# An RWKV-7 / Mamba-2 / HGRN2 encoder step on one core: four order changes in the RWKV tile, and the finest HGRN level built from the gate

## The chip, the core and the metric

One Trainium2 chip, one of its cores. The metric is the device time of one launch in microseconds (us). TensorE is called PE, VectorE DVE, ScalarE ACT, GpSimd POOL and SyncE SP, as in the profile.

## What is computed

Two layers over a prompt of 1,024 tokens and 8 sample sequences of 16 tokens (1,152 columns, nine tiles of 128; the ninth holds the samples). Layer 0 mixes with RWKV-7 and Mamba-2 side by side, layer 1 with HGRN2; each mixer is followed by a gated feed-forward block. The change touches the RWKV scan and the HGRN2 block:

```python
def rwkv7_scan(r, decay, k, v, kk, a, s0):      # per token
    sa = einsum('bhvk,bhk->bhv', s, -kk_t)
    s = s * d_t + sa[..., None] * (kk_t * a_t) + v_t[..., None] * k_t
    o_t = einsum('bhvk,bhk->bhv', s, r_t)

def hgrn2_mixer(p, s0, lb, norm_w, chunk):
    log_f = log(lb + (1 - lb) * sigmoid(f))
    k = (1 - lb) * sigmoid(-f)                  # so exp(log_f) = 1 - k
    o = gla_chunked(silu(q), k, i, log_f, s0, chunk)

def gla_chunked(q, k, v, log_f, s0, chunk):
    seg = bcum[l] - bcum[s]                     # bcum: running sum of log_f
    att[l, s] = sum_k q[l] * k[s] * exp(seg)    # s <= l
```

## The kernel before

The stages follow one another: modulation, input projection of layer 0, RWKV (about 560 to 925 us of the span), Mamba-2, output projection, feed-forward, input projection of layer 1, HGRN2 (about 2,550 to 2,850 us), output projection, feed-forward, final norm. In every stage each engine runs a list written out by hand, strictly in order; semaphores alone join the lists. What an engine does in which order is thus the order of the calls in its loop.

**RWKV.** The loop over tiles is a pipeline of three: in step t the engines work on the solve of tile t, the state and output of tile c = t-1, and the gates and keys of tile u = t+1. Names that matter:
- `tilde(u)` (DVE, L2338 to 2345) makes the scaled operands AR, kt and bt; its semaphore `tilde_done` releases `grams(t)` on PE (L2510), which multiplies bt with AR (L2518), AR with bt (L2523) and, after `bonus_done`, kt with AR (L2529).
- `mask_grams(t, True)` (DVE) masks the first two products; `square(t)` (PE, L2536 through the helper `product`) squares them; `take_powers(t)` (ACT, L2069) copies the squares out of PSUM. `mask_grams(t, False)` masks the key product (L2278) and then adds the identity (L2283, semaphore `T0_done`). `fourth(t)` on PE needs the identity sum, the copies and, since it writes over banks 2 and 3, the masked key product.
- `solve(c, 0)` (PE, L2623) and its copy `take_U(c, 0)` (ACT, L2064) belong to the tile before; ACT issues `take_U` ahead of `take_powers`.
- Five additions `add_T` (DVE, L2290) build the inverse. Between the second and third of them DVE does `finish(c-1)` (L2369 to 2375) and `keys(u)` (L2308, L2310).
- `tokens(t)` (PE, L2569) turns v, b and k; `take_tokens(t)` (ACT, L2080) copies the three in that order under one semaphore, `tok_done`. `state_rows(c, 1)` (PE, L2615) and `lora(u)` (PE, L2472) wait for it.
- `bonus_key(u)` (DVE, L2335) needs POOL's `kmod`; `add_o(c)` (L2357), `unit_k(u)` (L2328) and `centre(c)` (L2361, L2364) follow it. `unit_k` waits for ACT's `exps(u)` (L2114, L2116), which stands behind ACT's copies of the second cross product (L2086).

**HGRN2.** Attention inside a tile is split in levels 64, 32, 16, 8, 4, 2, 1. For a level m, ACT exponentiates sums of log_f that PE makes (`exponents`, L3847; `decays`, L3583) into the buffer E, in groups of three arrays: rem, cum, 64; then 32, 16, 8; then 4, 2, 1. DVE multiplies the lower half of each pair by k and the upper by q (`level`, L3707, two instructions), and PE multiplies that array with itself (`far_of`, L3873; `gram_of`, L3891). DVE picks the scores with masks (`far_scores`, `scores` L3745, `near_scores` L3755); `outputs` on PE (L3932, L3934) needs them. `turn_gate(u)` (L3966) waits until all of group three is exponentiated; then come ACT's copy (L3589), DVE's `low_part` (L3676), and with `lf_low` PE's exponents of the next tile. DVE's list for a tile reads: three levels, `new_state` (L3765), `finish(c)` (L3783, L3787), `level(t, 4)`, `far_scores`, `low_part`, `scores(t, 0)`, `level(t, 2)`, `level(t, 1)`, `scores` 1 to 3, `near_scores`.

SP loads k and q of tile u into `kqg[:, u % 2]` once `KQ_done`, `Qe_done` and `gram0` say that tile u-2 is through with them. After the last prompt tile POOL builds V_e (L3661, eight instructions) in the same buffer, behind the same three semaphores.

## Time and profile before

| | |
|---|---|
| median of 3 runs | 3790.82 us (3788.09 to 3794.73) |
| profiled execution, its own time | 3792.62 us |
| its span | 3790.6 us |
| PE busy | 3557.4 us, 94% |
| DVE busy | 2127.6 us, 56% |
| ACT busy | 1059.7 us, 28% |
| POOL busy | 1417.3 us, 37% |
| mean granted PE clock | 0.972 |

The busy shares are averages over stages with different limits. In a timeline row the first number is the start from the beginning of the span, the second the time until the group of instructions ends, and the bracket the idle time of that engine ahead of the group with the instruction that ended it. Groups overlap by a little because an engine starts an instruction before the last one has drained.

### The profile page before, as it was taken

What the parts mean: (1) busy time and instruction counts of PE and PEld (TensorE: products, weight loads), DVE (VectorE), ACT (ScalarE), POOL (GpSimd) and SP (SyncE); (2) the same over time, 40 slices, a digit from 0 to 9 for tenths busy, and PEclk for the clock granted to TensorE, in tenths of its full rate; (3) what the DMA queues carried; (4) which work ended last, traced back from release to release, by engine and by line L of the source; (5) the groups of instructions that cost most, each with busy time, mean ns of one, the idle gap of its engine ahead of it and who ended that gap; (6) DMA issues with size and microseconds to landing.
All of it is one profiled execution on the core that took longest, in us unless ns stands there. A gap on an engine that the chain in (4) does not pass through costs nothing. (4 is left out here: it accounts for less than half of the span.)

```text
span 3790.6 us, 69437 instructions
## 1 busy us (share of the span) xinstructions
PE 3557.4 (94%) x29702; PEld 3351.9 (88%) x29702; DVE 2127.6 (56%) x2992; ACT 1059.7 (28%) x1751; POOL 1417.3 (37%) x1140
## 2 busy tenths in 40 slices
PE   7999988888898999999999999988879899999998
PEld 6999967777668899999999999987769799999998
DVE  5543656664694675555644635337765855555446
ACT  2000114553551143333200224015540433332100
POOL 4222221210003367777533322230013577776331
PEclk8999999998899999999999999999999999999999
DMA  6454441001432112222322123223341122223322
GB/s 219 163 183 168 165 129 31 23 23 30 97 82 76 32 61 73 70 70 70 120 92 76 49 100 126 94 90 105 86 132 48 44 72 70 74 72 98 104 89 73
DMA packets 393333, 339.27 MB, mean 90 GB/s; under 512 B 19827, under 2 KB 363377, under 8 KB 386910
## 3 DMA queue, kind: packets, MB, share of 16 engines
q1 hardware_dynamic: 381712, 290.89, 25.0%
q10 hardware_dynamic: 11214, 44.33, 2.9%
q8 instruction: 215, 3.52, 0.4%
q0 software_dynamic: 128, 0.00, 0.2%
q14 instruction: 64, 0.52, 0.0%
HBM read 249.95 MB, written 85.24 MB: 88 GB/s over the span
## 5 line engine op out<-in xcount | busy, mean ns | idle before, releaser
L1301 PE MATMUL ffn_acc<-ffn_BH,ffn_WH 128*128 128x384 f32 x1232 | 418.8, 340 | 23.5 <-DVE ffn_BL L1511 12.6
L1301 PE MATMUL ffn_acc<-ffn_BL,ffn_WH 128*128 128x384 f32 x1232 | 417.0, 338 | 0.0
L1301 PE MATMUL ffn_acc<-ffn_BH,ffn_WL 128*128 128x384 f32 x1232 | 416.5, 338 | 0.0
L1238 POOL TENSOR_TENSOR ffn_WL<-raw,ffn_WH 128x512 fp32r<-128x512 f32 x176 | 282.3, 1606 | 261.5 <-ACT ffn_WH L1387 261.5
L1728 PE MATMUL ffn_acc<-ffn_BH,ffn_WH 128*128 128x384 f32 x1056 | 354.0, 335 | 6.7 <-DVE ffn_BL L1792 4.3
L1728 PE MATMUL ffn_acc<-ffn_BL,ffn_WH 128*128 128x384 f32 x1056 | 353.6, 335 | 0.0
L644 PE MATMUL in_ab_acc<-hH,in_ab_wH 128*128 128x384 f32 (+2 forms) x840 | 289.0, 344 | 5.1 <-DVE hL L502 5.1
L1238 POOL TENSOR_TENSOR ffn_WL<-ffn_S,ffn_WH 128x512 fp32r<-128x512 f32 x176 | 274.5, 1570 | 33.0 <-ACT ffn_WH L1387 33.0
L644 PE MATMUL in_ab_acc<-hL,in_ab_wH 128*128 128x384 f32 (+2 forms) x840 | 285.5, 340 | 0.0
L644 PE MATMUL in_c_acc<-hH,in_c_wH 128*128 128x384 f32 (+1 forms) x768 | 261.0, 340 | 6.9 <-DVE hL L502 6.8
L1301 PEld LDWEIGHTS ffn_acc<-ffn_BH,ffn_WH 128*128 128x128 f32 x1232 | 234.1, 190 | 30.9 <-POOL ffn_WL L1238 15.1
L644 PE MATMUL in_c_acc<-hL,in_c_wH 128*128 128x384 f32 (+1 forms) x768 | 260.7, 339 | 0.0
L1301 PE MATMUL ffn_acc<-ffn_hH,ffn_WH 128*128 128x394 f32 x704 | 239.8, 341 | 4.8 <-DVE ffn_hL L1543 4.3
L1301 PE MATMUL ffn_acc<-ffn_hH,ffn_WL 128*128 128x394 f32 x704 | 240.8, 342 | 0.0
L1301 PE MATMUL ffn_acc<-ffn_hL,ffn_WH 128*128 128x394 f32 x704 | 240.5, 342 | 0.0
L1728 PE MATMUL ffn_acc<-ffn_BH,ffn_WL 128*128 128x384 f32 x1056 | 240.4, 335 | 0.0
L1801 DVE SCALAR_TENSOR_TENSOR xT<-ffn_acc,mod,xT 128x768 f32<-128x768 f32 x96 | 97.6, 1016 | 254.3 <-PE ffn_acc L1728 254.3
L1301 PEld LDWEIGHTS ffn_acc<-ffn_BL,ffn_WH 128*128 128x128 f32 x1232 | 234.3, 190 | 0.0
L1301 PEld LDWEIGHTS ffn_acc<-ffn_BH,ffn_WL 128*128 128x128 f32 x1232 | 234.2, 190 | 0.0
L1728 PEld LDWEIGHTS ffn_acc<-ffn_BH,ffn_WH 128*128 128x128 f32 x1056 | 198.7, 188 | 7.9 <-DVE ffn_BL L1792 4.9
L1728 PEld LDWEIGHTS ffn_acc<-ffn_BL,ffn_WH 128*128 128x128 f32 x1056 | 198.7, 188 | 0.0
L644 PE MATMUL in_ab_acc<-hH,in_ab_wL 128*128 128x384 f32 (+2 forms) x840 | 196.6, 339 | 0.0
(629 smaller groups left out, 8210.7 us busy)
## 6 DMA issues: line engine op xcount, KB each, us to landing
in_ab_ada<-in_ada_w SPq DMA_DIRECT2D x40, 1024.0 KB, 5.0
hidden<-ffn_up SPq DMA_DIRECT2D x44, 576.0 KB, 2.8
raw<-in_w_gate SPq DMA_DIRECT2D x44, 512.0 KB, 3.7
raw<-in_w_up SPq DMA_DIRECT2D x44, 512.0 KB
raw<-in_w_down SPq DMA_DIRECT2D x80, 256.0 KB, 2.6
pT<-in_ab_out ACTq DMA_DIRECT2D x34, 576.0 KB, 3.2
pT<-in_c_out ACTq DMA_DIRECT2D x32, 576.0 KB, 3.7
raw<-in_w_in_ab SPq DMA_DIRECT2D x34, 512.0 KB, 4.5
```

What stands on the lines that cost most here:

```text
L644: ins = self.nc.tensor.matmul(self.acc[0:rows, u, c, 0:n], w[:, u, k, 0:rows], x[:, k, c * CH:c * CH + n], start=(k == 0 and w is self.wH ...
L1238: self.nc.gpsimd.tensor_tensor(self.WL[:, slot], src, self.WH[:, slot].bitcast(F32), ALU.subtract).then_inc(lo, 1)
L1301: ins = self.nc.tensor.matmul(self.acc[:, bank, 0:n], w[:, slot, k, :], x(low, k), start=start and k == 0 and w is self.WH and low == 0, s ...
L1728: ins = nc.tensor.matmul(acc[:, pair + c if c < 2 else third, 0:CH], w[:, slot, k, :], x[:, k, chunk(c)], start=k == 0 and w is m.WH and x ...
L1801: stt(xs, acc[:, pair:pair + 2, 0:CH], gate[:, n, 0:1], xs, ALU.mult, ALU.add)
```

## The change

In RWKV, DVE makes bt before kt, with a semaphore of its own for kt (`keys_done`), adds the identity before it masks the key product, and from tile 2 on does `bonus_key` after `add_o` (for tile 1 after `unit_k`). ACT copies the squares before `take_U(c, 0)`. The copy of v gets a semaphore (`v_copied`), for which `state_rows(c, 1)` now waits.

In HGRN2 the third group has two arrays. Level 1 is built by one DVE instruction as (1 - k) q in the upper half, and its product takes k itself as the other operand. Since k is thus read until that product is done, SP's load and POOL's V_e wait for `gram_mm` as well.

```diff
-            def take_powers(t):
+            def take_squares(t):
                 for q in range(2):
                     act.wait_ge(S1_mm, 2 * t + q + 1)
                     copy(flat4(pw[:, q, 0:2, :, :]), bank[:, q, :]).then_inc(S1_out, 1)
+
+            def take_powers(t):
...
-                for dst, b in ((v_tok, 6), (b_tok, 2), (k_tok, 3)):
-                    ins = copy(dst[:, t % 2, :, :, :].rearrange("p j q k -> p (j q k)"), bank[:, b, :])
-                ins.then_inc(tok_done, 1)
+                copy(tokens_of(v_tok), bank[:, 6, :]).then_inc(v_copied, 1)
+                copy(tokens_of(b_tok), bank[:, 2, :])
+                copy(tokens_of(k_tok), bank[:, 3, :]).then_inc(tok_done, 1)
...
+                if 0 <= t <= LAST:
+                    take_squares(t)
                 if 0 <= c < LAST:
                     take_U(c, 0)
...
-                tt(kt[:, :, :], kmod[:, :, :], c_[:, :, :], ALU.mult)
                 dve.wait_ge(ba_done, u + 1)
                 tt(bt[:, :, :], a_[:, :, :], c_[:, :, :], ALU.mult).then_inc(tilde_done, 1)
+                tt(kt[:, :, :], kmod[:, :, :], c_[:, :, :], ALU.mult).then_inc(keys_done, 1)
...
                 if front:
                     decay(u)
-                if front and u:
-                    bonus_key(u)
...
                 if 0 <= c <= LAST:
                     add_o(c)
+                if front and u > 1:
+                    bonus_key(u)
                 if front:
                     unit_k(u)
-                if u == 0:
+                if front and u <= 1:
                     bonus_key(u)
...
                 ins.then_inc(A_mm, 1)
+                pe.wait_ge(keys_done, t + 1)
                 pe.wait_ge(bonus_done, t + 1)
...
                 if s == 1:
-                    pe.wait_ge(tok_done, min(c + 2, NT))
+                    pe.wait_ge(v_copied, min(c + 2, NT))
...
-        GROUPS = (("rem", "cum", 64), (32, 16, 8), (4, 2, 1))
-        LAST_GROUPS = (("rem", "cum", 8), (4, 2, 1))
+        GROUPS = (("rem", "cum", 64), (32, 16, 8), (4, 2))
+        LAST_GROUPS = (("rem", "cum", 8), (4, 2))
...
                     sp.wait_ge(gram0, u - 1)
+                    sp.wait_ge(gram_mm, 4 * (u - 1))
...
             pool.wait_ge(gram0, NTP)
+            pool.wait_ge(gram_mm, 4 * NTP)
...
+            def level_1(t):
+                dve.wait_ge(E_done, NP * t + PAIRS_ * len(groups_of(t)))
+                v, k, q = (halves(x, 1)[1] for x in (buffer_of(t, 1), k_[:, t % 2], q_[:, t % 2]))
+                stt(v, k, 1.0, q, ALU.subtract, ALU.mult, reverse0=True).then_inc(KQ_done, 1)
...
-                            ins = mm(bank[:, b + h % 2, 0:3 * P], lf_tok[:, part, h, :], sums_r[:, at:at + 3, :],
+                            ins = mm(bank[:, b + h % 2, 0:n * P], lf_tok[:, part, h, :], sums_r[:, at:at + n, :],
...
+                keys_ = k_[:, t % 2] if FINE[i] == 1 else KQ
```

DVE's list in step t of RWKV from the key product on, before (`act` holds the powers and masked products, `mixer_shared` the state S):

```order
L2296 TENSOR_TENSOR sumsq<-sumsq,rwkv_bank 64x512
L2278 TENSOR_TENSOR act<-rwkv_bank,rwkv_mask_k 128x512 x2
L2283 TENSOR_TENSOR act<-act 128x256 x2
L2290 TENSOR_TENSOR act<-act,rwkv_bank 128x256 x2
L2301 TENSOR_TENSOR mixer_shared<-mixer_shared,rwkv_bank 128x256
```

and of the change:

```order
L2301 TENSOR_TENSOR sumsq<-sumsq,rwkv_bank 64x512
L2283 TENSOR_TENSOR act<-act 128x256 x2
L2287 TENSOR_TENSOR act<-rwkv_bank,rwkv_mask_k 128x512 x2
L2295 TENSOR_TENSOR act<-act,rwkv_bank 128x256 x2
L2306 TENSOR_TENSOR mixer_shared<-mixer_shared,rwkv_bank 128x256
```

The identity sums (L2283 in both) have moved ahead of the two key masks. ACT's list at the same place, before:

```order
L2064 COPY rwkv_Ut<-rwkv_bank 64x512
L2069 COPY act<-rwkv_bank 128x512 x2
L2072 COPY rwkv_W<-rwkv_bank 128x512 x2
L2075 COPY act<-rwkv_bank 128x256 x2
L2090 ACTIVATE rwkv_tanh_in<-act 64x128
```

and of the change:

```order
L2069 COPY act<-rwkv_bank 128x512 x2
L2064 COPY rwkv_Ut<-rwkv_bank 64x512
L2074 COPY rwkv_W<-rwkv_bank 128x512 x2
L2077 COPY act<-rwkv_bank 128x256 x2
L2093 ACTIVATE rwkv_tanh_in<-act 64x128
```

The two copies of the squares (L2069) now stand ahead of the copy of U.

## Rows read from the trace of the kernel before

**Rows 1.** Busy time by stretch: RWKV's steady tiles, and most of HGRN2.
```profile
604.70:900.00 295.30, 261.63 (x6594) 230.56 (x6591) 194.55 (x357) 148.58 (x312) 51.19 (x42) 1.00 0.08 22
...
2500.00:2800.00 300.00, 261.43 (x4793) 232.58 (x4793) 195.68 (x347) 139.10 (x163) 29.17 (x54) 0.97 0.34 100
```
**Rows 2.** Timeline of PE, a steady RWKV tile.
```profile
682.29 1.10 PE L2518 MATMUL rwkv_bank<-rwkv_AR,rwkv_bt 64*64 64x128 f32 x32 [0.86 <-DVE rwkv_bt L2345]
...
687.52 1.09 PE L2623 MATMUL rwkv_bank<-sumsq 64*64 64x64 f32 x16
689.81 0.39 PE L2536 MATMUL rwkv_bank<-act 64*64 64x64 f32 x6 [1.20 <-DVE act L2283]
...
698.80 0.68 PE L2615 MATMUL rwkv_bank<-mixer_shared,rwkv_AR 64*64 64x64 f32 x16 [0.67 <-ACT rwkv_k_tok L2080]
...
700.50 0.68 PE L2584 MATMUL rwkv_bank<-act 64*64 64x64 f32 x16
...
719.88 1.10 PE L2518 MATMUL rwkv_bank<-rwkv_AR,rwkv_bt 64*64 64x128 f32 x32 [0.86 <-DVE rwkv_bt L2345]
```
**Rows 3.** Timeline of DVE, the same tile, first half.
```profile
681.56 0.68 DVE L2345 TENSOR_TENSOR rwkv_bt<-raw 128x512 f32<-128x512 f32 x1
...
687.00 1.27 DVE L2278 TENSOR_TENSOR act<-rwkv_bank,rwkv_mask_k 128x512 f32<-128x512 f32 x2
688.20 0.74 DVE L2283 TENSOR_TENSOR act<-act 128x256 f32<-128x256 f32 x2
...
695.65 0.42 DVE L2290 TENSOR_TENSOR act<-act,rwkv_bank 128x256 f32<-128x256 f32 x1 [0.51 <-PE rwkv_bank L2536]
...
699.81 0.74 DVE L2290 TENSOR_TENSOR act<-act,rwkv_bank 128x256 f32<-128x256 f32 x2
```
**Rows 4.** Timeline of ACT, the same stretch.
```profile
681.01 0.84 ACT L2134 COPY sumsq<-rwkv_bank 128x256 f32<-128x256 f32 x2 [2.91 <-PE rwkv_bank L2599]
...
688.65 0.58 ACT L2064 COPY rwkv_Ut<-rwkv_bank 64x512 f32<-64x512 f32 x1 [3.08 <-PE rwkv_bank L2623]
689.13 1.06 ACT L2069 COPY act<-rwkv_bank 128x512 f32<-128x512 f32 x2
...
697.09 0.58 ACT L2080 COPY rwkv_v_tok<-rwkv_bank 128x512 f32<-128x512 f32 x1 [1.14 <-PE rwkv_bank L2569]
```
**Rows 5.** Timeline of DVE, second half of the tile.
```profile
710.75 2.13 DVE L2335 SCALAR_TENSOR_TENSOR rwkv_columns<-rwkv_columns,colB,rwkv_kmod 128x128 f32<-128x128 f32 x4 [1.10 <-POOL rwkv_kmod L2245]
...
714.16 0.69 DVE L2328 TENSOR_TENSOR rwkv_kk<-rwkv_kk,rwkv_sq 128x512 f32<-128x512 f32 x1 [0.68 <-ACT rwkv_sq L2116]
```
**Rows 6.** Timeline of ACT and POOL, second half of the tile.
```profile
710.48 0.58 ACT L2129 COPY rwkv_o<-rwkv_bank 128x512 f32<-128x512 f32 x1 [2.91 <-PE rwkv_bank L2658]
...
710.67 1.27 POOL L2235 TENSOR_TENSOR raw<-raw 128x512 f32<-128x512 f32 x1
```
**Rows 7.** Timeline of DVE, a steady HGRN tile.
```profile
2637.09 1.29 DVE L3707 TENSOR_TENSOR hgrn_E<-hgrn_E,hgrn_kqg 128x512 f32<-128x512 f32 x2 [0.58 <-ACT hgrn_E L3583]
...
2639.55 1.21 DVE L3676 TENSOR_TENSOR hgrn_lf_tok<-hgrn_bank,hgrn_lf_tok 128x1024 fp32r<-128x1024 f32 x1
```
**Rows 8.** Timeline of PE and ACT, the same HGRN tile.
```profile
2635.54 1.51 ACT L3583 ACTIVATE hgrn_E<-hgrn_bank 128x768 f32<-128x768 f32 x2 [0.63 <-PE hgrn_bank L3847]
...
2640.81 1.66 PE L3847 MATMUL hgrn_bank<-decay_sums,hgrn_lf_tok 128*128 128x384 f32 x8 [0.25 <-DVE hgrn_lf_tok L3676]
```
**Rows 9.** Timeline of DVE, level 4 of the first HGRN tile.
```profile
2576.11 1.29 DVE L3707 TENSOR_TENSOR hgrn_E<-hgrn_E,hgrn_kqg 128x512 f32<-128x512 f32 x2 [2.98 <-ACT hgrn_E L3583]
```
**Rows 10.** Timeline of POOL and DVE at the end of HGRN.
```profile
2788.32 4.61 POOL L3661 TENSOR_TENSOR hgrn_kqg<-raw,row_half 128x256 f32<-128x256 f32 x8 [246.60 <-DVE hgrn_E L3707]
2793.08 1.80 DVE L3755 COPY_PREDICATED act<-act 32x256 f32<-32x256 uint32 x4
...
2816.67 4.96 DVE L3755 COPY_PREDICATED act<-act 32x256 f32<-32x256 uint32 x4
2817.21 4.12 POOL L3667 TENSOR_TENSOR hgrn_late<-hgrn_late,act 128x1024 f32<-128x1024 f32 x2 [24.28 <-PE hgrn_bank L3948]
```

27 lines of the change are left out of this document (15 added, 12 removed).

## The prediction

> **What bounds the kernel now.** I read first the busy time by stretch, then the timelines of the two stages that the change touches, engine by engine, looking in each for the wait that ends last. The change touches nothing outside RWKV (about 560 to 925 us) and HGRN2 (about 2,550 to 2,850 us), so everything else is carried over as it is. In both stages PE is the busiest engine but not full: 262 of 295 us in the steady RWKV tiles, 261 of 300 in HGRN2 [rows 1]. PE waits there for chains through DVE and ACT, and only the waits on such a chain are worth anything.
>
> A steady RWKV tile takes 719.88 - 682.29 = 37.6 us from one gram product to the next [rows 2]; there are seven of them (tiles 1 to 7). PE has three waits in the first half: 0.86 us ahead of L2518 for bt, 1.20 us ahead of L2536 at 689.81, and 0.67 us ahead of L2615 for the last token copy [rows 2]. From 700.50 on PE runs without a gap up to the second cross product, then come ACT's copy of it, its Ln and its Exp, and from 714.16 DVE is the chain up to bt [rows 5].
>
> An HGRN tile takes about 28.8 us. The chain that I find is DVE's: it stands 0.58 us for the last exponential of group three, then does level 4, the far scores and `low_part`; PE stands 0.25 us for `low_part` [rows 7, 8]. From there PE's exponents and grams, DVE's near scores, PE's outputs and ACT's copy lead back to DVE.
>
> **RWKV, edit by edit (steady tile).**
>
> *bt before kt.* bt is finished one operation of 0.60 us earlier, at 681.64 instead of 682.24 [rows 3]. But the grams also need R to be copied out of banks 0 and 1, and these copies end at 681.01 + 0.84 = 681.85 [rows 4]. The new wait takes the place of the old one: L2518 starts near 681.9, gain 0.4 us (bounds 0 and 0.6). The key product stands behind `bonus_done` as before, and kt is ready before that, so `keys_done` costs nothing; if bonus were sooner, kt would end 0.6 us ahead of it still.
>
> *Identity first and squares before U, together.* What held PE until 689.81 was the last of three things: the identity sum, finished at 688.94 [rows 3], and the first copy of the squares, finished at 689.13 + 0.58 = 689.71 because ACT had waited until 688.65 for U [rows 4]. PE had its square products done by about 687.7, since it started the solve at 687.52 [rows 2]; with the copies in front both are out by about 688.3, before U is there at 688.65, so U is not delayed. On DVE the identity sums take 687.00 to 687.7 and the first key mask is done near 688.4, half of the 1.27 us later [rows 3]. PE is busy with the solve until 689.81 - 1.20 = 688.6 [rows 2]. So the fourth power can start at 688.6: gain 1.2 us (bounds 0.8, should the second key mask at 689.0 hold it, and 1.3). Each edit alone would give less: without the ACT edit the wait stays at 689.71.
>
> *`v_copied`.* L2615 needs only v, copied by 697.67 [rows 4], and can start when PE is through with the third product, 0.67 us before 698.80 [rows 2]. `lora` still waits for the last copy, which ended just before 698.80, so it starts there instead of 0.6 us later, behind L2615. But the cross product that follows needs the third addition on DVE, which starts at 699.81 because DVE had 3.7 us of `finish` and `keys` since 696.07 [rows 3]; the first half of it is there near 700.23. So L2584 moves from 700.50 to 700.28: gain 0.2 us (bounds 0 and 0.8).
>
> *`bonus_key` after `add_o`.* DVE waited 1.10 us for kmod and then took 2.13 us for four instructions, which end at 712.88 [rows 5]. POOL's L2235 runs from 710.67 to 711.94 [rows 6]. Moved, they come behind an addition of about 0.7 us that waits for ACT's copy of o, done at 711.06 [rows 6], and can start at 711.8. `unit_k` waits for ACT until 714.16 anyway. I cost the move at nothing; the cover is the 1.3 us between 712.88 and 714.16, and should the four instructions last their 2.13 us from 711.8, they end at 713.9, just inside. The mean comes 1.3 us earlier but DVE takes it only after `unit_k`. Bounds: 1.0 us lost if the cover goes, 0.6 gained.
>
> Per steady tile 0.4 + 1.2 + 0.2 = 1.8 us, seven times 12.6 us. In tile 8 the first two terms hold and the third does not (extra matmuls fill PE there): 1.6 us. In tile 0 there is no U; bt and the identity are worth about 0.9, and for u = 1 `bonus_key` now comes behind `unit_k` (0.6 us), with POOL running against it: about 0.5 lost, net 0.4. **RWKV: 14.6 us less.**
>
> **HGRN2, edit by edit.**
>
> *Group three with two arrays.* PE's eight matmuls of 384 columns took 1.66 us [rows 8]; 256 columns should leave 1.66 minus at most a third (0.55), at least nothing. I take 0.43, which is 8 times 128 columns at 2.4 GHz, the level of the granted 1.00 there. The exponential of 768 elements was 0.8 us (two in 1.51); a copy of 512 elements out of PSUM takes 0.58 [rows 4, 8], so 0.2 less for the one that ends last. The last exponential of the group comes 0.43 + 0.43 + 0.2 = 1.06 us earlier. DVE waited only 0.58 us for it [rows 7], then it is bound by its own list (`finish` before level 4). So a steady tile gains 0.58 us, and PE's other 0.5 us turn into a longer wait for `low_part`. Seven tiles: 4.1 us. In tile 0 there is no `finish` and DVE waited 2.98 us [rows 9]: the whole 1.06 counts.
>
> The Trainium skill (TensorE: Matmul & The Clock Gate, Back-to-back issue gap) gives a sustained spacing of about 81 ns at 128 columns and 131 ns at 512; by that rule 128 columns would be worth about 17 ns a matmul, 0.13 us per eight, the exponential would come 0.46 us earlier and a steady tile would gain 0.46, not 0.58 us. The row speaks for a steeper price, since eight matmuls of 384 columns in 1.66 us are some 0.17 us apart, beyond the page's figure for 512.
>
> *Level 1 by one instruction instead of two.* One DVE instruction of 0.6 us less, but in steady tiles DVE then waits for PE's last gram; covered by PE. In the last tile, where DVE leads, it and the smaller group give about 0.6 us. The product with k as the other operand costs the same number of matmuls.
>
> *The later load of k and q.* It is issued about 2.5 us later and needed a tile later: nothing.
>
> *V_e.* POOL's eight instructions (0.61 us each, 4.61 in all) ran 2788.32 to 2792.93, while DVE's near scores, on the chain, came at 2793.08 and took 1.80 us [rows 10]. Now POOL starts when the last gram is done, at the same moment as the near scores. One case shows what that costs: at 2816.67 the same four instructions took 4.96 us beside POOL's L3667 [rows 10]. Bounds 0 and 3.2 us, once; I take 2.4, four waits of one POOL instruction (0.61) each. The Trainium skill (SBUF — State Buffer, Who interferes with whom) says that a DVE instruction with two SBUF inputs and a POOL instruction that reads SBUF block each other for a whole instruction; by that rule it is the 2.4, by the ratio of the two rows 3.2. Here the change speaks against itself.
>
> **HGRN2: 4.1 + 1.1 + 0.6 - 2.4 = 3.4 us less.** Sum 14.6 + 3.4 = 18.0 us. The profiled execution took 3792.6, so its like would be 3774.6; the median of the runs is 1.8 us lower, which gives **3773 us**. A measurement of this kernel can tell about 0.2% (7.6 us) from no change, so faster begins below 3783.2.
>
> **The rivals.**
> - *The next wait gives half of RWKV back.* For: every gain there was already cut by a successor 0.2 to 0.4 us behind (R's copies, the solve on PE, `keys` on DVE), and durations of the key masks are modelled. If the fourth power starts only after the second mask, and bt and v are worth nothing, a tile gains 0.8 instead of 1.8: 7 us less gain, 3780 us. Chance 0.15.
> - *PE is the bound after all.* For: PE is busy nine tenths of both stages. Then the HGRN tile gains its whole 1.06 (3.4 us more) and the earlier mean in RWKV is worth up to 0.5 a tile (4 us): 3766 us. Against: the bracketed waits for DVE. Chance 0.10.
> - *The edits do not bite.* The identity and the key mask only change places, both being needed, and V_e takes what HGRN gives: 0.4 a tile left, about 3787 us, no change. Against: the ACT order, a clear 1 us. Chance 0.08.
> - *Slower, by PE's clock.* The leaner HGRN tile leaves PE with longer waits (0.25 becomes about 0.7 us ahead of the next exponents). The granted clock was 0.97 in this stretch, so it does fall there at times [rows 1]; 0.5 (1.2 GHz) would double PE's work. If a third of each of the seven tiles (about 10 us) ran at the lower level, it would cost 5 us a tile, 35 us in all: 3808 us. It decides once it takes 25 us more than now, about 3.6 us a tile. The same page on the clock gate has the clock fall after an idle window; that rule would give this case, and so far the trace has no fall in the steady tiles, whose longest PE waits are 1.2 us. Chance 0.04.
>
> **How the numbers follow.** My case has 0.63, with a range of its own of 3767 to 3780. With the first two rivals, faster is 0.88, same 0.08, slower 0.04. The range 3762 to 3784 takes in the first two rivals and the bounds of the RWKV terms, and leaves out the last two.
>
> **What would show it.** In the new profile: L2518 waiting for R's copies rather than bt; ACT's L2069 ahead of L2064 and the wait ahead of the fourth power gone; the RWKV tile at 35.8 us; the HGRN tile at 28.3 us with DVE's 0.58 us wait gone and PE's wait for `low_part` grown to about 0.7; near scores of the last prompt tile near 4 us beside V_e. I am wrong if the RWKV tile stays above 36.7 us, if the HGRN tile is a full microsecond shorter, or if the granted clock falls in steady tiles.

## Result, and the profile after

The changed kernel took 3762.61 us, median of the runs beside which the kernel before took 3792.06 us (four, 3788.09 to 3794.73). The ratio is 0.992, with a 95% interval of 0.9906 to 0.9934. (One of the changed kernel's four executions was disturbed, at a granted clock of 0.77, and is left out of the ratio.) So the gain was 29.5 us where 18.0 were forecast; 3762.61 lies at the very edge of the range (3762 to 3784), and 29.5 us less than the 3790.82 from which the forecast started would be 3761.3, outside it. Over every execution of this study the kernel before averages 3790.9 us (47 of them, 3781.2 to 3799.2) and the changed one 3763.5 (13, 3759.1 to 3770.4): a difference of 27.4 us, with a standard error of about 1.0. A single pair of profiles can be off by several microseconds either way, and much below turns on that.

The page of the changed kernel, its first lines:

```profile
span 3760.5 us, 69444 instructions
...
PE 3537.9 (94%) x29702; PEld 3338.3 (89%) x29702; DVE 2118.6 (56%) x2983; ACT 1053.5 (28%) x1751; POOL 1417.9 (38%) x1140
```

PE is busy 19.5 us less, DVE 9.0, ACT 6.2. Busy time fell by less than the span (30.1 us).

**The RWKV tile.** PE's timeline of a steady tile, answering to [rows 2] (start, duration, engine, line, operation, tiles, and in brackets the idle time ahead with what ended it):

```profile
677.55 1.10 PE L2523 MATMUL rwkv_bank<-rwkv_AR,rwkv_bt 64*64 64x128 f32 x32 [0.52 <-DVE rwkv_bt L2349]
...
682.77 1.09 PE L2629 MATMUL rwkv_bank<-sumsq 64*64 64x64 f32 x16
683.74 2.92 PE L2542 MATMUL rwkv_bank<-act 64*64 64x64 f32 x93
...
691.88 0.64 PE L2621 MATMUL rwkv_bank<-mixer_shared,rwkv_AR 64*64 64x64 f32 x14
692.72 0.34 PE L2477 MATMUL rwkv_bank<-rwkv_tanh_in,rwkv_w 64*128 64x128 f32 x1 [0.20 <-ACT rwkv_k_tok L2084]
```

All three waits of before have shrunk or gone: the one ahead of the first gram from 0.86 to 0.52 us, the 1.20 us ahead of the fourth power altogether, and the 0.67 us ahead of the cross product (L2621 now) has become 0.20 us in front of the low-rank products. The same tile on ACT and on DVE:

```profile
676.62 0.84 ACT L2137 COPY sumsq<-rwkv_bank 128x256 f32<-128x256 f32 x2 [2.90 <-PE rwkv_bank L2605]
...
681.58 0.58 ACT L2069 COPY act<-rwkv_bank 128x512 f32<-128x512 f32 x1 [0.40 <-PE rwkv_bank L2542]
682.98 0.58 ACT L2069 COPY act<-rwkv_bank 128x512 f32<-128x512 f32 x1 [0.82 <-PE rwkv_bank L2542]
683.90 0.58 ACT L2064 COPY rwkv_Ut<-rwkv_bank 64x512 f32<-64x512 f32 x1 [0.33 <-PE rwkv_bank L2629]
```

```profile
676.56 0.68 DVE L2349 TENSOR_TENSOR rwkv_bt<-raw 128x512 f32<-128x512 f32 x1
677.17 0.68 DVE L2350 TENSOR_TENSOR rwkv_kt<-rwkv_kmod,raw 128x512 f32<-128x512 f32 x1
...
682.24 0.75 DVE L2283 TENSOR_TENSOR act<-act 128x256 f32<-128x256 f32 x2
682.91 1.27 DVE L2287 TENSOR_TENSOR act<-rwkv_bank,rwkv_mask_k 128x512 f32<-128x512 f32 x2
```

The bracket ahead of L2523 names DVE's bt, which ends at 677.24. ACT's second copy of R ends later, at 676.62 + 0.84 = 677.46, and PE starts at 677.55: the bracket names one of several semaphores, and the durations show which was last. The copies of the squares wait for PE alone now, the second done at 683.56, before the fourth power at 683.74.

**The HGRN tile.** I cut it in three on DVE: from the first addition into the state (L3765 before, L3780 after) to `low_part` (L3676, L3686), from there to the near scores (L3755, L3770), and on to the next addition. A steady tile before:

```profile
2631.96 2.15 DVE L3765 SCALAR_TENSOR_TENSOR hgrn_S<-hgrn_S,act,hgrn_bank 128x128 f32<-128x128 f32 x8
...
2646.54 1.80 DVE L3755 COPY_PREDICATED act<-act 32x256 f32<-32x256 uint32 x4
...
2660.80 2.15 DVE L3765 SCALAR_TENSOR_TENSOR hgrn_S<-hgrn_S,act,hgrn_bank 128x128 f32<-128x128 f32 x8
```

and after:

```profile
2607.25 2.15 DVE L3780 SCALAR_TENSOR_TENSOR hgrn_S<-hgrn_S,act,hgrn_bank 128x128 f32<-128x128 f32 x8
...
2611.72 1.29 DVE L3722 TENSOR_TENSOR hgrn_E<-hgrn_E,hgrn_kqg 128x512 f32<-128x512 f32 x2
...
2614.16 1.21 DVE L3686 TENSOR_TENSOR hgrn_lf_tok<-hgrn_bank,hgrn_lf_tok 128x1024 fp32r<-128x1024 f32 x1
...
2621.47 1.81 DVE L3770 COPY_PREDICATED act<-act 32x256 f32<-32x256 uint32 x4
...
2635.33 1.89 DVE L3780 SCALAR_TENSOR_TENSOR hgrn_S<-hgrn_S,act,hgrn_bank 128x128 f32<-128x128 f32 x7
```

With `low_part` at 2639.55 [rows 7] the parts were 7.59, 6.99 and 14.26 us; now they are 6.91, 7.31 and 13.86 us. The first part hardly varies in the steady tiles, 7.58 to 7.61 us in four profiles before and 6.90 to 6.92 after, since DVE no longer stands in front of level 4 (L3722). In the first period, where DVE waited 2.98 us [rows 9], it went from 7.59 to 6.48. The other two parts vary from tile to tile, 6.4 to 10.7 and 13.85 to 19.3 us: a second thing is at work there, which a section below takes up.

On PE the pieces of the forecast:

```profile
2609.38 1.21 PE L3862 MATMUL hgrn_bank<-decay_sums,hgrn_lf_tok 128*128 128x256 f32 x8
...
2614.41 0.75 PE L3907 MATMUL hgrn_bank<-hgrn_E 128*32 128x32 f32 x64 [0.40 <-DVE act L3748]
2615.42 1.68 PE L3862 MATMUL hgrn_bank<-decay_sums,hgrn_lf_tok 128*128 128x384 f32 x8 [0.26 <-DVE hgrn_lf_tok L3686]
```

Eight matmuls of 256 columns take 1.21 us, 0.45 less than of 384 [rows 8] (forecast 0.43). PE's wait for `low_part` stayed at 0.26 us; the half microsecond that was to lengthen it lies 1 us earlier, as a new 0.40 us wait for DVE's far scores.

**The end of HGRN2**, answering to [rows 10]:

```profile
2766.11 6.32 POOL L3671 TENSOR_TENSOR hgrn_kqg<-raw,row_half 128x256 f32<-128x256 f32 x8 [243.84 <-PE hgrn_bank L3907]
```

```profile
2766.46 2.82 DVE L3770 COPY_PREDICATED act<-act 32x256 f32<-32x256 uint32 x4
```

V_e and the near scores do run side by side, and both suffer: POOL's eight instructions 6.32 us instead of 4.61, DVE's four 2.82 instead of 1.80. The cost on the chain was 1.0 us, not 2.4.

### The profile page after: what moved, and what is told of

Read it like the earlier page. It is cut to its first block and busy times, and to the rows that moved or that the text cites. A ratio compares the mean times of both kernels' runs of the same rounds, so it can differ in the third digit from the quotient of the medians.

```text
span 3760.5 us, 69444 instructions
## 1 busy us (share of the span) xinstructions
PE 3537.9 (94%) x29702; PEld 3338.3 (89%) x29702; DVE 2118.6 (56%) x2983; ACT 1053.5 (28%) x1751; POOL 1417.9 (38%) x1140
## 3 DMA queue, kind: packets, MB, share of 16 engines
q1 hardware_dynamic: 381712, 290.89, 25.5%
## 5 line engine op out<-in xcount | busy, mean ns | idle before, releaser
L644 PE MATMUL in_ab_acc<-hH,in_ab_wH 128*128 128x384 f32 (+2 forms) x840 | 289.1, 344 | 5.1 <-DVE hL L502 5.1
L644 PE MATMUL in_ab_acc<-hL,in_ab_wH 128*128 128x384 f32 (+2 forms) x840 | 285.3, 340 | 0.0
L644 PE MATMUL in_c_acc<-hH,in_c_wH 128*128 128x384 f32 (+1 forms) x768 | 261.3, 340 | 6.8 <-DVE hL L502 6.8
L644 PE MATMUL in_c_acc<-hL,in_c_wH 128*128 128x384 f32 (+1 forms) x768 | 261.2, 340 | 0.0
L644 PE MATMUL in_ab_acc<-hH,in_ab_wL 128*128 128x384 f32 (+2 forms) x840 | 196.5, 339 | 0.0
```

The lines of the kernel that those rows point to most:

```text
L644: ins = self.nc.tensor.matmul(self.acc[0:rows, u, c, 0:n], w[:, u, k, 0:rows], x[:, k, c * CH:c * CH + n], start=(k == 0 and w is self.wH ...
```

## The part of the first 30 us that no edit explains

Against the same instructions in both first profiles, the change was 14.2 us ahead at RWKV's last grams and 15.5 at the transposes behind RWKV (L2914), which nothing in it touches. There (from before's L2914 to its L2938) the kernel before took 19.47 us and the changed one 15.29, so it was 19.7 us ahead. HGRN2's seven periods brought it to 24.8, and what lies behind them to 30.1. This gave two theories, **C**: the stretches of low granted clock fall differently in every execution, and **D**: it belongs to the edits.

## The experiments

### Each stage alone

`rwkv_only` has the RWKV part of the diff, `hgrn_only` the HGRN2 part.

> The RWKV edits alone, HGRN2 as before. My theory: the RWKV tile stays at 35.67 us as in the changed kernel, RWKV is 15.7 us shorter at tile 8's fourth power, and HGRN2 keeps its 28.85 us tile; the rest of what is gained comes from where PE's granted clock stands low between RWKV and Mamba-2, 4.5 us in the changed kernel, which may be here again or not. Sum 3771 to 3776 us (16 to 21 less than before). Rival: the gain outside the two stages belongs to the HGRN edits; then this is 16 us and hgrn_only has all the rest.

> The HGRN2 edits alone, RWKV as before. My theory: 6 us less in HGRN2 (the tile 28.85 to 28.1 us, 1.1 us in tile 0, V_e costs about 1), nothing before it, so 3784 to 3787 us; the stretch between RWKV and Mamba-2 stays as long as in the kernel before, since RWKV ends at the same time. If the gain of 3.6 us behind HGRN2 follows the clock's phase, it may differ from the changed kernel's. Rival: the sum of the two halves is far from the whole 29.5 us because the edits help each other: then this one gives less than 3 us or more than 10.

`rwkv_only`: 3774.47 us, ratio 0.9949 (0.9934 to 0.9964), against 3791.73 for the kernel before. RWKV tile 35.67 us. `hgrn_only`: 3778.36 us, ratio 0.9964 (0.9951 to 0.9977); RWKV tile 37.58 us. The two give 17.3 and 13.4 us, 30.7 together, so within their intervals (13.6 to 25.0 and 8.7 to 18.6 us) they add up. HGRN2's part, forecast at 3.4 and expected here at 6, is beyond its rival's bound of 10 and the larger surprise; its own profile has 9.4 us of it inside HGRN2. In `hgrn_only`'s profile L2914 to L2938 took 15.27 us although nothing ahead of it differs from the kernel before, the first sign for theory C.

### The group of three arrays back, all else changed

```diff
-        GROUPS = (("rem", "cum", 64), (32, 16, 8), (4, 2))
-        LAST_GROUPS = (("rem", "cum", 8), (4, 2))
+        GROUPS = (("rem", "cum", 64), (32, 16, 8), (4, 2, "spare"))
+        LAST_GROUPS = (("rem", "cum", 8), (4, 2, "spare"))
```

> The changed kernel, but PE and ACT still make and exponentiate the third array of group three, which nobody reads (DVE overwrites it with level 1 from the gate). My theory: DVE's wait of 0.58 us ahead of level 4 is back in each HGRN tile and the tile is 28.6 to 28.7 us, so the smaller group is worth 0.6 us a tile and the single DVE instruction almost nothing there. Rival (PE bound): the tile stays near 28.85, since PE's 0.9 us are back; rival (DVE's instruction count): it stays at 28.1.

One execution, 3771.41 us. DVE's timeline, a steady tile:

```profile
2639.60 2.15 DVE L3780 SCALAR_TENSOR_TENSOR hgrn_S<-hgrn_S,act,hgrn_bank 128x128 f32<-128x128 f32 x8
...
2644.73 1.29 DVE L3722 TENSOR_TENSOR hgrn_E<-hgrn_E,hgrn_kqg 128x512 f32<-128x512 f32 x2 [0.59 <-ACT hgrn_E L3592]
2647.20 1.21 DVE L3686 TENSOR_TENSOR hgrn_lf_tok<-hgrn_bank,hgrn_lf_tok 128x1024 fp32r<-128x1024 f32 x1
```

The wait is back (0.59 us, 0.58 before), and the first part of the tile is 7.60 us. The two-array group alone makes that part shorter; level 1 by one instruction, the other thing left in, does nothing to it. Four periods took 28.1 to 28.8 us, the three others 30.0 to 31.8.

### The two losing edits mended

```diff
-                if front and u > 1:
+                if front and u:
                     bonus_key(u)
...
-                if front and u <= 1:
+                if u == 0:
                     bonus_key(u)
...
-            pool.wait_ge(gram_mm, 4 * NTP)
+            pool.wait_ge(att_done, NTP)
```

> The changed kernel with two places mended: for tile 1 bonus_key stands ahead of unit_k as before, and POOL starts V_e only when the near scores of the last prompt tile are done. My theory: tile 0 of RWKV is about 1.5 us shorter, the last outputs of HGRN2 come 1.0 us earlier (near scores 1.8 instead of 2.8 us); 2.5 us less, 3760 us, if the low stretches of PE's clock fall alike. Rival: those stretches move with the shift and hide it: 3758 to 3766.

3760.29 us, ratio 0.9913 (0.9899 to 0.9926). RWKV's tile 0 took 33.49 us instead of 35.10, and the near scores of the last prompt tile 1.79 us again, with POOL behind them (its eight instructions took 7.43 us there, beside other work of DVE, and nothing waited for them). It was timed again at the end (below).

### The same kernels again: what one execution can show

> The kernel before, profiled a second time. What is disputed is the time outside the two changed stages: from RWKV's last products to Mamba-2 the change took 4.5 us less, and another 3.6 us after HGRN2, though no instruction differs there. Theory C (where the stretches of low granted clock fall differs from one execution to the next): the stretch from the first transposes behind RWKV (L2914) to the last ones (L2938) lasts anything from 15.3 to 19.5 us here, not 19.47 again, and the span differs from the first by up to 5 us. Rival D (the gain outside belongs to the edits): 19.47 us again within 0.3, span 3790.6 within 2.

> The changed kernel, profiled a second time. The stretch from L2914 to L2938 (before's numbering) took 15.29 us in its first profile. Theory C: anything from 15.3 to 19.5 us. Rival D: 15.3 within 0.3. Both expect RWKV tiles of 35.67 us within 0.05, and HGRN tiles whose irregular gaps (2.3 us in the fourth tile of the first profile) may lie in another tile.

> The changed kernel once more, in rounds beside the kernel before. The pairs of profiles differ: 30.1 us between the first two, 19.9 between the second two. Theory C (about 5 us of the first difference was where the low clock happened to fall): the difference of medians is 22 to 27 us. Rival (the 30 us are the change's): 28 to 31 us. Between: L2914 to L2938 (before's numbering) 15.3 us in most executions.

`before_again` 3784.91 us, `after_again` 3764.89; `after_third` 3766.06 us in the median, ratio 0.9934 (0.9913 to 0.9955). The stretch from L2914 to L2938, by window (us; PE, PEld, DVE, ACT, POOL busy with their instructions; granted PE clock, DMA share, GB/s), in the first profile before, in `before_again`, in the first after, and in `after_third`:

```profile
937.40:956.87 19.47, 17.25 (x91) 12.32 (x91) 5.05 (x6) 12.05 (x20) 0.00 (x0) 0.59 0.64 164
```

```profile
934.43:949.70 15.27, 12.10 (x90) 8.40 (x91) 5.05 (x6) 11.78 (x20) 0.00 (x0) 0.88 0.83 209
```

```profile
921.91:937.20 15.29, 12.10 (x90) 8.42 (x91) 5.06 (x6) 11.77 (x20) 0.00 (x0) 0.89 0.84 209
```

```profile
921.59:941.05 19.46, 17.25 (x91) 12.25 (x91) 5.06 (x6) 12.06 (x20) 0.00 (x0) 0.59 0.65 164
```

Both kernels have both cases: 15.3 us at a mean granted clock of 0.88, and 19.5 us at 0.59. The clock rows of the traces have two levels, 1.00 (2.4 GHz) and 0.5 (1.2 GHz), so about a quarter of the stretch was at the lower in the one case and four fifths in the other, and PE's 91 matmuls took 12.1 or 17.2 us. Theory C holds here, D falls. This stretch alone moved the first comparison by 4.2 us. What decides between the two cases is not shown.

### One RWKV edit undone at a time

All start from the changed kernel and have one execution each: `no_squares` 3780.07 us (3771 expected), `no_identity` 3766.02, `no_bt` 3765.89, `no_v` 3762.78, `old_bonus` 3759.02. The changed kernel's own executions lie from 3759.1 to 3770.4, so these times decide little, and I go by the RWKV tile. `no_squares`:

```diff
-                if 0 <= t <= LAST:
-                    take_squares(t)
                 if 0 <= c < LAST:
                     take_U(c, 0)
                 if 0 <= t <= LAST:
+                    take_squares(t)
                     take_powers(t)
```

> The changed kernel with ACT's copies of the squares behind U again, as before. My forecast gave the ACT order and the identity order 1.2 us together and said that neither works without the other. So: the wait ahead of the fourth power is back, near 1.1 us, ended by ACT, and the RWKV tile is 36.8 us (36.6 to 37.0), time 3771 us. Rival (the identity order alone carries it): tile 36.0 or less.

The RWKV tile took 37.00 us, 1.33 more, at the upper end of what was expected. (The time was 16.5 us above the changed kernel's mean where the tiles account for 9.2; 3.2 more are the stretch from L2914 to L2938, 19.50 us here.) PE's timeline, fourth power, where the wait has no semaphore in the bracket; ACT's shows what is late:

```profile
687.22 2.92 PE L2541 MATMUL rwkv_bank<-act 64*64 64x64 f32 x93 [1.20 <-issue]
```

```profile
686.06 0.58 ACT L2064 COPY rwkv_Ut<-rwkv_bank 64x512 f32<-64x512 f32 x1 [2.72 <-PE rwkv_bank L2628]
686.54 1.06 ACT L2069 COPY act<-rwkv_bank 128x512 f32<-128x512 f32 x2
```

The first square is out at 686.54 + 0.58 = 687.12, and PE starts at 687.22. The profile calls this wait "issue", but the engine that it waits for is ACT.

`no_identity` puts the masks of the key product ahead of the identity sums again:

```diff
-                dve.wait_ge(gram_out, 2 * t + 2)
-                for q in range(2):
-                    ins = tt(pw[:, q, 2, :, :], gram_b[:, b, q, :, 0, :], bc(eye[:, :], 1, PAIRS), ALU.add)
-                ins.then_inc(T0_done, 1)
                 for q in range(2):
                     dve.wait_ge(gram_k_mm, t + 1)
...
+                dve.wait_ge(gram_out, 2 * t + 2)
+                for q in range(2):
+                    ins = tt(pw[:, q, 2, :, :], gram_b[:, b, q, :, 0, :], bc(eye[:, :], 1, PAIRS), ALU.add)
+                ins.then_inc(T0_done, 1)
```

> The changed kernel with the identity sums behind the key masks again on DVE. My forecast: the fourth power then waits for the identity sum behind two masks of 1.27 us, as before near 1.2 us after PE is through with the solve: RWKV tile 36.7 us (36.3 to 36.9). Without squares first it was 37.00. Rival (ACT's order alone does it): 35.9 or less.

36.20 us, 0.52 more, below what I expected (36.7, with 36.3 as the lower bound): PE waits 0.38 us ahead of the fourth power, since the sums end soon after PE gets there.

```profile
685.30 2.95 PE L2542 MATMUL rwkv_bank<-act 64*64 64x64 f32 x93 [0.38 <-DVE act L2288]
```

Without the ACT order the DVE order seems to have no worth: both undone were not run, but what the other two edits leave of the whole 1.90 us (0.35 and 0.22, below) is the same 1.33. With the ACT order, the DVE order brings 0.52 of the 1.33.

`no_bt` has kt ahead of bt again, `no_v` lets the cross product wait for all three copies again:

```diff
+                tt(kt[:, :, :], kmod[:, :, :], c_[:, :, :], ALU.mult).then_inc(keys_done, 1)
                 dve.wait_ge(ba_done, u + 1)
                 tt(bt[:, :, :], a_[:, :, :], c_[:, :, :], ALU.mult).then_inc(tilde_done, 1)
-                tt(kt[:, :, :], kmod[:, :, :], c_[:, :, :], ALU.mult).then_inc(keys_done, 1)
```

```diff
-                    pe.wait_ge(v_copied, min(c + 2, NT))
+                    pe.wait_ge(tok_done, min(c + 2, NT))
```

> The changed kernel with kt ahead of bt again. My forecast: 0.4 us a tile, so 36.1 us (35.7 to 36.3), the wait ahead of the grams (L2518 in before's numbering) being for bt, 0.6 us later than now. Rival (the copies of R or of the identity chain hold it anyway): 35.7 to 35.8.

> The changed kernel with L2615 (before's numbering) waiting for all three token copies again. My forecast: 0.2 us a tile (bounds 0 and 0.8): RWKV tile 35.9 us. The other undone parts measured 37.00 without the ACT order, 36.20 without the DVE order, 36.03 without bt first, 35.69 with bonus_key at its old place, beside 35.68 changed and 37.58 before; 1.90 less 1.33 less 0.35 leaves 0.22 for this one. Rival (the cross product waits for the same copies anyway): 35.7.

36.03 us (0.35) and 35.90 us (0.22). PE's waits came back, here for the grams and for the cross product:

```profile
678.82 1.10 PE L2523 MATMUL rwkv_bank<-rwkv_AR,rwkv_bt 64*64 64x128 f32 x32 [0.87 <-DVE rwkv_bt L2350]
```

```profile
694.12 0.68 PE L2621 MATMUL rwkv_bank<-mixer_shared,rwkv_AR 64*64 64x64 f32 x16 [0.67 <-ACT rwkv_k_tok L2084]
```

`old_bonus` has `bonus_key` ahead of `add_o` again:

```diff
+                if front and u:
+                    bonus_key(u)
                 if c == LAST:
...
-                if front and u > 1:
-                    bonus_key(u)
                 if front:
                     unit_k(u)
-                if front and u <= 1:
+                if u == 0:
                     bonus_key(u)
```

> The changed kernel with bonus_key at its old place, ahead of add_o. My forecast costed the move at nothing in a steady tile and at 0.5 us lost in tile 0. So: RWKV tile 35.67 us within 0.1, DVE waiting about 1.1 us for kmod ahead of bonus_key again, and tile 0 shorter by 0.5 (forecast) or by about 2 us (what the trace of the changed kernel suggests: tile 0 took 35.10 us though 1 us was gained at its start). Rival (the later place delays unit_k or helps the mean): the tile changes by over 0.2 us either way.

35.69 us, as with the change: the move is worth nothing in a steady tile. Tile 0 took 33.78 us instead of 35.10. `bonus_key(1)` in the changed kernel, then here:

```profile
596.41 0.71 DVE L2333 TENSOR_TENSOR rwkv_kk<-rwkv_kk,rwkv_sq 128x512 f32<-128x512 f32 x1 [2.00 <-ACT rwkv_sq L2119]
597.05 3.15 DVE L2340 SCALAR_TENSOR_TENSOR act<-act,colB,rwkv_kmod 128x128 f32<-128x128 f32 x4
```

```profile
596.20 2.12 DVE L2340 SCALAR_TENSOR_TENSOR act<-act,colB,rwkv_kmod 128x128 f32<-128x128 f32 x4 [2.21 <-POOL rwkv_kmod L2250]
598.25 0.68 DVE L2333 TENSOR_TENSOR rwkv_kk<-rwkv_kk,rwkv_sq 128x512 f32<-128x512 f32 x1
```

It starts 0.85 us later, and its four instructions last 1.03 us longer. One by one they took 1.35, 1.35, 0.34 and 0.34 us in the changed kernel and 1.33, 0.34, 0.34 and 0.34 here: an instruction of 0.34 us that runs beside one of POOL's (L2240, L2253, 1.3 to 1.7 us) lasts a whole microsecond longer, and at the later place two of them do, not one. PE's bonus sums wait for them (L2509 at 600.26, at 598.38 here).

### What the irregular gaps in HGRN2 are

PE's waits in HGRN2's seven periods before have lines with "issue": idle time within a string of small matmuls for which no semaphore stands.

```profile
PE hgrn_bank L3891 <- issue: 3.9, 5, 2.2
...
PE hgrn_bank L3859 <- issue: 2.6, 4, 0.8
PE hgrn_bank L3847 <- issue: 2.4, 1, 2.4
```

With one more of 0.25 the gaps sum to 9.2 us there; in four profiles before 9.2, 11.0, 11.3 and 15.4, in four after 10.1, 11.1, 10.4 and 11.0. The seven periods lasted 205.7, 209.5, 211.0 and 213.8 us before. The largest gaps of the changed kernel come at the very same matmul in each of its four profiles, with 22 of a string's 64 left (first profile, then `after_fourth`):

```profile
2648.03 0.39 PE L3907 MATMUL hgrn_bank<-hgrn_E 128*32 128x32 f32 x22 [2.33 <-issue]
```

```profile
2647.13 0.39 PE L3907 MATMUL hgrn_bank<-hgrn_E 128*32 128x32 f32 x22 [2.32 <-issue]
```

The DMA view of the gap between, 2645.5 to 2648.1, shows a packet of the instruction queue among the load's:

```profile
q1 hardware_dynamic: 482, 0.24, 32.0%
q8 instruction: 1, 0.02, 2.3%
```

Two theories, both tried. **L**: the loads matter. The change's later load of k and q, which I had costed at nothing, parts them. The kernel before with that one wait added:

```diff
                     sp.wait_ge(gram0, u - 1)
+                    sp.wait_ge(gram_mm, 4 * (u - 1))
```

> The kernel before, and of the change only the one added wait on SP's queue in HGRN2: the load of k and q starts after the last gram. My forecast costed it at nothing: 3791 us, within 2 of the kernel before. New theory L: the load is where HGRN2 gained more than forecast. In the traces PE stands 0.6 to 3.8 us without a semaphore in strings of small gram matmuls, next to the 16 KB packets of the instruction queue q8, and most where these come while the loads run back to back (2.5 MB in 10 us). With the later load the 1.5 MB and the 1.0 MB come apart in every tile. By L the seven periods of HGRN (first add into the state to the eighth) fall from 205.7 to 210.7 us (three profiles with the old order) to about 204, and the time is 3 to 5 us less. An own effect of the new order beyond 6 us would surprise both.

3786.31 us, ratio 0.9991 (0.9981 to 1.0002), the kernel before 3789.49 beside it. The seven periods took 206.9 us where 204 were expected (the mean of four profiles before: 210.0), gaps 9.9 us, and the first part of the tile stayed at 7.59. In the time the interval holds no change. In the traces one gap settles more, the one between the matmuls of L3847 in the sixth period, in the kernel before and in `load_only`:

```profile
2736.24 0.62 PE L3847 MATMUL hgrn_bank<-decay_sums,hgrn_lf_tok 128*128 128x384 f32 x2 [2.40 <-issue]
```

```profile
2729.65 0.62 PE L3848 MATMUL hgrn_bank<-decay_sums,hgrn_lf_tok 128*128 128x384 f32 x2 [1.03 <-issue]
```

The 2.5 us ahead of these gaps, by window, before and in `load_only` (the last two numbers are the DMA share and GB/s):

```profile
2731.30:2733.80 2.50, 2.50 (x128) 2.18 (x127) 1.71 (x4) 0.49 (x2) 0.00 (x0) 1.00 1.14 343
```

```profile
2726.10:2728.60 2.50, 2.50 (x128) 2.17 (x127) 1.72 (x4) 0.22 (x1) 0.00 (x0) 1.00 0.20 38
```

(A packet that begins in the window counts whole, so the share can pass 1.) In all five profiles with the early load this gap is 2.40 to 3.77 us, in all fifteen with the later load 1.02 to 2.13; with RWKV's edits it stands five matmuls earlier in the string. So the later load shortens the gap of the sixth period; the sixth period of `load_only` took 29.67 us, those of the kernel before 30.7 to 33.9. For the other gaps it is not shown.

**I**: the gaps sit where packets of PE's instructions end. `shift64` was to add half a packet's worth of matmuls to tile 0:

```diff
-                        ins = mm(near_bank(4)[r, h, :], k_[:, t % 2, h, r], q_[:, t % 2, h, r], start=True, stop=True)
+                        for _ in range(3 if t == 0 else 1):
+                            ins = mm(near_bank(4)[r, h, :], k_[:, t % 2, h, r], q_[:, t % 2, h, r], start=True, stop=True)
```

> The changed kernel with each of the 32 first gram products (L3874) of HGRN2's tile 0 done three times: 64 matmuls more, 128 records of PE's instruction stream, half of a 16 KB packet, worth 2 to 3 us once at most. Theory I (the gaps in PE's strings without a semaphore sit where the instruction packets end): in three profiles of the changed kernel the periods that stand out are the fourth (30.1 to 31.3 us) and the sixth (29.4 to 30.3) of seven, the others near 28.0; here both go back to 28.5 or less, others may stand out instead, and the gap of 1.8 to 2.6 us in the fourth is gone. Rival (the gaps belong to loads or to tiles): fourth and sixth stand out again, by 1.5 us or more.

3768.63 us. The fourth period, 30.1 to 31.3 us in the changed kernel, took 27.62, and the gap of 2.3 us in it was gone. The sixth still stood out (29.48 us) with its gap of 1.86 us. Another gap of 3.08 us stood within the tripled string.

This run does not test I, because it shifted by a whole packet and not by half of one. The 64 extra products are 128 matmuls in the profile (29,830 instead of 29,702) and 128 weight loads more, and the instruction queue q8 moved 216 packets instead of 215. So the ends of the packets fell on the same matmuls as in the changed kernel, and so did the gaps: tile 0's stands with 6 of the string left in both, here of 2.37 us and there of 1.39 to 1.82 (first profile of the changed kernel, then `shift64`).

```profile
2561.79 0.26 PE L3907 MATMUL hgrn_bank<-hgrn_E 128*32 128x32 f32 x6 [1.39 <-issue]
```

```profile
2568.95 0.26 PE L3908 MATMUL hgrn_bank<-hgrn_E 128*32 128x32 f32 x6 [2.37 <-issue]
```

That the fourth period's gap was gone says nothing for the shift either: it was gone in `no_v` too (27.60 us), which adds no matmul.

What speaks for I is in the traces of the other runs. First, each of the 223 gaps above 0.2 us in the twenty profiles, the last prompt tile included, ends 1.2 to 1.6 us after a packet of 16 KB on q8 has landed; the sixth period's is no exception. Second, the gaps lie 127 or 128 matmuls apart or near a multiple of that (380, 508), and 128 matmuls with their weight loads are the 256 instructions that made one packet in `shift64`. Third, RWKV's edits move them though they touch nothing in HGRN2: tile 0's string had 2 matmuls left in the kernel before, in `hgrn_only` and in `load_only`, and 6 in `rwkv_only` and the changed kernel, and the fourth period's 18 left in `hgrn_only`,

```profile
2662.71 0.35 PE L3901 MATMUL hgrn_bank<-hgrn_E 128*32 128x32 f32 x18 [2.00 <-issue]
```

and 22 in the changed kernel. (The wait for `keys_done`, nine of them, would by my estimate shift the stream by nine instructions, four to five pairs of matmul and weight load.) So in these traces a gap stands only where a packet ends. How long it is at such a place, from nothing to 3.8 us, depends on the load in one case and is open in the others.

**What follows a large gap.** Within the seven periods PE's clock fell to its lower level for 3.4 us (once for 6.8), once or twice in each of the four profiles of each kernel. Each time it fell within a gap of 1.8 to 2.95 us or at most 1.6 us behind its end: at 2585.3 us in the first profile before, at 2649.1 in the first after, where the gap of 2.33 us ends at 2648.03. Other gaps as long had no fall behind them. Its price shows in the sixth period of `after_again` and of `after_fourth`, with the same gap of 1.85 us: the third part took 15.43 us at the full clock and 17.05 with such a stretch. Taking the gaps and half of the time at the lower clock from the seven periods leaves (us):

| profile | seven periods | gaps | lower clock | left |
|---|---|---|---|---|
| `before` | 205.7 | 9.2 | 3.4 | 194.8 |
| `before_again` | 209.5 | 11.0 | 6.8 | 195.1 |
| `before_third` | 211.0 | 11.3 | 10.2 | 194.6 |
| `before_fourth` | 213.8 | 15.4 | 6.8 | 195.0 |
| `after` | 201.5 | 10.1 | 3.4 | 189.7 |
| `after_again` | 202.2 | 11.1 | 3.4 | 189.4 |
| `after_third` | 202.1 | 10.4 | 3.4 | 190.0 |
| `after_fourth` | 202.9 | 11.0 | 3.4 | 190.2 |

What is left is the same within 0.8 us for each kernel and differs by 5.0 us, close to the 5.2 of the first part of the tile (0.69 us in six, 1.11 in the first). The gaps give 1.1 us more and the clock 1.7, 7.8 in all.

### The size, and the sum of the stages

> The changed kernel beside the kernel before once more, in five rounds, for the size. By the stages of the profiles the change is worth 23.3 us: 13.4 up to RWKV's last grams, 1.3 in its last tile, 6.8 in HGRN2's seven periods, 1.8 behind them. By that the difference of the medians is 21 to 26 us. Rival (something outside the two stages that three profiles on each side do not show): 28 to 31 us.

> The kernel before, profiled once more. All its times so far average 3790.7 us (38 of them), its two profiles have spans of 3790.6 and 3783.0 (3786.8, or 3788.7 as a time); those of the changed kernel average 3763.5 (13 of them). The stages of the profiles give 23.3 us of the 27.2. If the missing 4 us are the sample of two profiles, this one and the next have spans near 3790 with the extra in the stretches that no edit touches (L2914 to L2938 at 19.5 instead of 15.3 us, the feed-forward, the end) or in HGRN2's seven periods (208.6 us); if a changed stage was read too low, it shows there.

> As for the run ahead of it: the kernel before, profiled a fourth time, for the mean of each stage: RWKV to the last grams 297.7 us within 0.3 whatever the span is, HGRN2's seven periods 205 to 211 us.

`after_fourth`: 3763.16 us against 3792.41, ratio 0.9921 (0.9908 to 0.9935), 29 us, nearer to the rival than to my 21 to 26. `before_third` took 3788.87 us, `before_fourth` 3793.56. With four profiles of each kernel the means of the stages are (us):

| stage | before | after | difference |
|---|---|---|---|
| to the first grams | 571.8 | 571.4 | -0.4 |
| first to last grams of RWKV | 297.7 | 284.5 | -13.2 |
| to L2914 | 66.9 | 65.9 | -1.0 |
| L2914 to L2938 | 16.4 | 16.3 | -0.1 |
| to HGRN2's first addition | 1613.6 | 1612.3 | -1.3 |
| its seven periods | 210.0 | 202.2 | -7.8 |
| to the end | 1011.7 | 1009.9 | -1.8 |
| span | 3788.1 | 3762.6 | -25.5 |

So two profiles of before had been too few: its HGRN2 was read too short (`before_fourth`, at 213.8 us, is beyond the 205 to 211 that I expected). The table is 25.5 us, the times of all executions 27.4 with an error of 1.0; the 1.3 us in the fifth line is less than that stage's own spread (1611.4 to 1614.1).

> The changed kernel with bonus_key(1) ahead of unit_k again and V_e behind att_done, timed once more. The stages: 1.1 us in RWKV's tile 0 and 0.5 us at HGRN2's end, so about 1.6 us less than the changed kernel, 3761 to 3763 us. Rival: nothing that can be told from it, 3763.5 or more.

3757.66 us (3754.69 to 3761.75) where 3761 to 3763 were expected, ratio 0.9909 (0.9893 to 0.9926). Its nine executions average 3759.5 us with an error of 1.0, 4 us below the changed kernel's 3763.5. It is the fastest version here, though of the 4 us only about 1.4 in tile 0 and 0.8 behind HGRN2's last period show in the stages.

## Why the prediction was right in its direction and wrong in its size

**The step that failed is the sum for HGRN2.** It was 4.1 + 1.1 + 0.6 - 2.4 = 3.4 us; the stages measured 9.2 (7.8 in the seven periods, 1.4 behind them). Two of its terms were mis-sized and one was missing. V_e, priced at 2.4 us lost, cost 1.0. The smaller group gave 0.69 us a tile for 0.58. And PE's idle time that no semaphore explains, with the lower clock behind it, was carried over as it was, with the later load of k and q at "nothing"; this gave 2.6 us in the seven periods and 1.1 in the last prompt tile.

- **RWKV, forecast 14.6 us: right.** First to last grams measured 13.2. In tile 8 PE's output product (L2658) came 1.4 us earlier behind the grams, of which the mean keeps 1.0 up to L2914, where PE's clock fell at different places. The steady tile went from 37.57 to 35.68 us, 1.9 for a forecast 1.8: bt first 0.35 (0.4), the two orders together 1.33 (1.2), v 0.22 (0.2), `bonus_key` 0. R's copies are what PE now waits for, as said. That the sum came out so well is in part luck: tile 0 was 0.8 us short of its term, and tiles 1 to 7 gave 13.7 us for 12.6, tile 1 alone 2.3. That each edit alone would give less held too: ACT's order alone gives 0.8 of the 1.33, and DVE's alone, by the sum above, nothing.
- **Tile 0, forecast 0.4 gained: wrong by 0.8.** It took 34.6 us before, 35.0 after and 33.6 mended (means of four, four and three profiles). So the start was worth 1.0 us (0.9 forecast), and the step that failed here is "about 0.5 lost": the later `bonus_key(1)` cost 1.4 us, since at its new place two of its four instructions meet one of POOL's and not one (3.15 instead of 2.12 us), beside its later start. I had named the meeting with POOL and priced only the order.
- **HGRN2's group, forecast 0.58 a tile and 1.06 once: right, a little low.** The part of the tile that holds it shrank by 0.69 us in each of six tiles and by 1.11 in the first: 5.2 us of the 7.8.
- **HGRN2's other 2.6 us: no term of mine holds them.** I took for constant what was not: the gram strings hold 9 to 15 us of gaps without a semaphore, of which I had read one profile and priced none. By the table above the gaps were 1.1 us shorter and the stretches at the lower clock behind them cost 1.7 us less (2.8 by this count). "The later load of k and q: nothing" is the step that is shown wrong in part, by the sixth period's gap. RWKV's edits and their shift of the packets are the other thing that moves gaps. How much of the 2.6 is each one's, and how much chance, stays open.
- **V_e, forecast 2.4 us lost: mis-sized.** It measured 1.0 us in the near scores and 0.8 by mending it. I had taken the neighbour with larger POOL instructions (two of 128x1024, [rows 10]) as a guide; four waits of a whole POOL instruction each did not come. The Trainium skill (SBUF — State Buffer, Who interferes with whom) has such pairs block each other for a whole instruction; by that, four meetings would be the 2.4 us, and the trace agrees that both are slowed but gives 0.25 us for each of the four.
- **The last tiles.** The time from the last prompt tile's first addition to the next projection (L644) went from 69.6 to 68.1 us where my terms made it 1.2 us longer (0.58 and 0.6 gained, 2.4 lost). The near scores of the last prompt tile came 1.65 us earlier behind that addition: the group's 0.69, and gaps of 1.1 us instead of 2.2. The sample tile gained 0.8, and V_e took 1.0.
- **The columns.** The price of 128 columns was 0.45 us for eight matmuls, as reckoned from the granted clock, not the 0.13 which the Trainium skill's spacing (TensorE: Matmul & The Clock Gate, Back-to-back issue gap) would make it.
- **The rivals.** "PE is the bound after all" gave 3766 and came closest in time, but not by its mechanism: PE still waits for `low_part`, and the part in front of it shrank by 0.69, not 1.06 us. The rivals above 3773 did not come. The slower case by PE's clock was argued from a misreading: the longest PE wait in HGRN2's tiles was not 1.2 but 2.40 us, in the sixth period, and the clock does fall behind such gaps. But it fell for less time in the changed kernel (3.4 us in each profile, 3.4 to 10.2 before), so this worked for the change and not against it.

Of the 9.4 us between the mean of all executions (27.4) and the forecast, HGRN2 accounts for 5.9 (3.3 in the seven periods, 2.6 behind them), and RWKV's two stages for -0.4. Another 2.0 us lie in stages that no edit touches, and 1.9 between the four profiles of each kernel and all executions. These last two stay open, and so does what part of the first comparison's 29.5 was chance.

## What to carry to other kernels

Price the idle time in front of an instruction, but profile the same kernel more than once before trusting any stretch: here two executions of the same code differ by 4 us in one 15 us stretch and by 8 us in one stage. An edit that "only" moves a load or a helper's start is a term with a price, the more if it meets another engine. Before a test by a shifted instruction stream is read, count in its profile by how much it shifted. When moves on two engines feed one wait, undo each by itself: here one of them carried most of it.

## What the runs showed of the hardware that was not expected

- A stretch of 91 small matmuls took PE 12.1 us at a mean granted clock of 0.88 and 17.2 us at 0.59, and which of the two came changed between executions of identical code.
- Strings of small matmuls (0.75 us for 64) and the matmuls between them stop for up to 3.77 us with no semaphore, only where a 16 KB packet of PE's instructions ends: each such gap ends 1.2 to 1.6 us after a packet has landed, and an edit in another stage moved the places by 4 to 5 matmuls. With DMA traffic of 343 GB/s ahead of it one such gap was 2.40 us, with 38 GB/s 1.03.
- Behind some of the large gaps PE's clock was at its lower level for 3.4 us, which cost 1.6 us in one tile.
- A DVE instruction of 0.34 us lasted 1.35 beside a POOL instruction (`bonus_key(1)`), and this happened to two of four. Four near scores went from 0.45 to 0.70 us each in the mean, while POOL's own eight went from 4.61 to 6.32 us.
